# A two-layer encoder on one core: the end of a layer by token tile, a reordered first stage, two more expert weights beside the ring, attention values by pair

## What is computed

```python
h = rms_norm(x, mix_norm_g[l])
aq, ak, av, bq, bk, bv, cq, ckv, ckr, gates = split(h @ w_in[l])
x += sum_n(sigmoid(gates_n) * (branch_n(h) @ w_branch[l, n])) @ w_out[l]
x += cross_attention(rms_norm(x, cross_norm_g[l]), rms_norm(mem, mem_norm_g[l]))
x += moe(rms_norm(x, ffn_norm_g[l]))   # 32 experts, top 2 of one group of 8
```

## Time and profile before

| | us |
|---|---|
| median of three runs (lowest, highest) | 1718.87 (1715.06, 1721.05) |
| the profiled execution | 1717.54 |
| its span, first to last instruction | 1715.4 |
| TensorE busy, share of the span | 1375.3, 80% |
| VectorE, ScalarE, GpSimd busy | 531.1, 231.5, 35.0 |
| moved by DMA | 505.57 MB, 295 GB/s on average |

### The profile page before, as it was taken

The page is one execution under the profiler, slowest core; times in us unless marked ns, Lnnn a source line. Parts: engine busy times, 40 slices in busy tenths (PEclk is TensorE's granted clock), DMA queues, the critical chain, the costliest instruction groups (busy, mean ns, idle before and its releaser), DMA issues.

```text
span 1715.4 us, 18172 instructions
## 1 busy us (share of the span) xinstructions
PE 1375.3 (80%) x7588; PEld 824.1 (48%) x7588; DVE 531.1 (31%) x1042; ACT 231.5 (13%) x552; POOL 35.0 (2%) x45
## 2 busy tenths in 40 slices
PE   5999999998666556777689999999986665676665
PEld 5887688854222123232258776887542121322211
DVE  5134646435111311221121345643432211212122
ACT  2013330022000000000011144100310000000000
POOL 2000000001000000000000000000000000000000
PEclk9999999999887878798889999999998787888888
DMA  9843227445999999999995332454489999999995
GB/s 310 270 140 99 74 70 246 157 178 217 408 421 421 422 420 421 421 421 421 421 348 171 111 111 69 118 215 168 172 324 421 421 422 421 418 421 421 422 422 234
DMA packets 137925, 505.57 MB, mean 295 GB/s; under 512 B 8688, under 2 KB 80176, under 8 KB 88432
## 3 DMA queue, kind: packets, MB, share of 16 engines
q1 hardware_dynamic: 134288, 492.98, 73.8%
q0 software_dynamic: 2704, 8.22, 1.5%
q10 hardware_dynamic: 848, 3.15, 0.5%
HBM read 503.27 MB, written 1.05 MB: 294 GB/s over the span
## 4 chain that ended last, share of the span: by engine, by line
PE 55%; DMA 39%; DVE 2%; SPq 2%; issue 1%; ACT 1%; POOL 0%; DVEq 0%; ACTq 0%; POOLq 0%
DMA ring<-in_w_dram 37%; PE banks L1435 26%; PE banks L1622 6%; PE banks L1662 5%; PE banks L1441 4%; PE banks L1734 3%; SPq L487 2%; PE banks L1546 1%; PE banks L1556 1%; PE banks L1582 1%; DMA k<-in_w_xkv_dram 1%; PE banks L1542 1%; PE banks L1591 1%; PE banks L1720 1%; PE banks L1487 0%
## 5 line engine op out<-in xcount | busy, mean ns | idle before, releaser
L1622 PE MATMUL banks<-ring,v 128*32 128x512 f32 x1936 | 302.9, 771 | 188.7 <-DMA ring<-in_w_dram 180.9
L1435 PE MATMUL banks<-hT,ring 128*128 128x256 f32 (+1 forms) x1472 | 327.6, 383 | 1.9 <-ACT hT L617 1.9
L1435 PEld LDWEIGHTS banks<-hT,ring 128*128 128x128 f32 (+1 forms) x1472 | 277.5, 190 | 48.4 <-issue 5.0
L1622 PEld LDWEIGHTS banks<-ring,v 128*32 128x32 f32 x1936 | 81.8, 136 | 397.1 <-issue 393.0
L1662 PE MATMUL banks<-ring,probT 128*32 128x512 f32 x1024 | 154.5, 730 | 88.3 <-DMA ring<-in_w_dram 80.0
L1662 PEld LDWEIGHTS banks<-ring,probT 128*32 128x32 f32 x1024 | 40.8, 131 | 190.4 <-issue 179.9
L1171 DVE COPY q<-banks 128x512 f32<-128x512 f32 x16 | 11.1, 692 | 246.6 <-PE banks L1662 246.6
L1591 PE MATMUL banks<-v,h 128*128 128x128 f32 x512 | 68.5, 297 | 13.3 <-issue 11.9
L1591 PEld LDWEIGHTS banks<-v,h 128*128 128x128 f32 x512 | 65.0, 209 | 27.2 <-issue 27.2
L1167 DVE TENSOR_TENSOR prob<-banks,prob 128x512 f32<-128x512 f32 x16 | 11.1, 692 | 205.6 <-PE banks L1622 205.6
L1160 DVE TENSOR_SCALAR prob<-prob 128x512 f32<-128x512 f32 x16 | 6.8, 427 | 184.8 <-ACT prob L698 184.8
(11 more groups left out here) (261 smaller groups left out, 1282.2 us busy)
## 6 DMA issues: line engine op xcount, KB each, us to landing
ring<-in_w_dram SPq DMA_DIRECT2D x370, 1024.0 KB, 19.1
ring<-in_w_in_dram SPq DMA_DIRECT2D x52, 1024.0 KB, 11.9
ring<-in_w_branch_dram SPq DMA_DIRECT2D x8, 1024.0 KB, 5.1
ring<-in_w_out_dram SPq DMA_DIRECT2D x8, 1024.0 KB, 5.9
k<-in_w_xkv_dram POOLq DMA_DIRECT2D x4, 1024.0 KB, 17.8
ring<-in_w_branch_dram SPq DMA_DIRECT2D x8, 512.0 KB, 3.5
k<-in_w_dram SPq DMA_DIRECT2D x4, 1024.0 KB, 8.6
shared<-in_w_dram SPq DMA_DIRECT2D x4, 1024.0 KB, 6.3
```

Of the source, the lines that this page charges most:

```text
L1435: last = nc.tensor.matmul(dst, w[:, k, cols], src[:, k, :], start=k == 0, stop=k == kn - 1)
L1622: last = nc.tensor.matmul(bank[2 + m][e * CAP:(e + 1) * CAP, :], xt[:, k, e * CAP:(e + 1) * CAP], ws[e][:, r * D_EXPERT:(r + 1) * D_EXPERT ...
```

## The change

It has five parts.

1. **Layer's end.** In the last round the four products go tile by tile (tile 0 both halves, then tile 1) into four PSUM banks (`END_BANKS`), so none waits for an addition. ScalarE squares each half as it is added; 1/rms is made by the half-tile form; GpSimd multiplies `x` by the norm weight, chunk by chunk, ahead of 1/rms, and the factor is put in by ScalarE (tile 0, and the first half of tile 1) and VectorE (the second half of tile 1). The norm weight is loaded by GpSimd's queue during the first round, no longer before it.
2. **TensorE filled in the joint** between the layers: four matmuls on the identity after the products, and one after the transposes of each tile.
3. **First stage.** The identity part of the constants and both `mem` weights go first on SyncE's queue; positions, the other constants and the lambdas after three ring loads. `mem` is turned over unnormed; its norm weight is put in as a factor per partition with the copies out of PSUM, and 1/rms by a multiplication of the keys with a row (made by two more matmuls on `ones` and a diagonal) and of the values with a column. The 24 setup steps come after `hT` is copied, the values' product after the transposes of `h`. Identity matmuls stand ahead of and between the transposes of `mem`.
4. **Beside the ring** there are 9 blocks: the first two w2 blocks of the first round are added, one in `prob` and a half of `probT`, one in `gain` and `oa`. What used these tiles in that time is moved to `q1` and `v1`. SyncE's queue gets two more waits: for all products of attention, and for GpSimd's four multiplications.
5. **Values by pair.** Both query tiles of a unit are multiplied at once: 12 products of 256 columns in place of 24 of 128 in A, B and C. Odd units keep their turned probabilities in `gain`, for which reason the FFN norm weight is loaded later.

```diff
+END_BANKS = (5, 2, 0, 1)
-EXTRA = 7
+EXTRA = 9
+AHEAD = [KD + i for i in range(7)] + [2 * KD, 2 * KD + 1]
...
-        act_e, act_r, hidden = flat
+        act_e, hidden = yexp[:, 0:512], yexp[:, 512:1024]
+        extras = [[e] for e in extras]
+        extras += [[prob[:, :, :, :].rearrange("p b a n -> p (b a n)"), probT[:, 1, :, :, :].rearrange("p a b n -> p (a b n)")],
+                   [gain[:, :], oa[:, :, :].rearrange("p c n -> p (c n)")]]
+        memT = shared[:, 0:SLOT].rearrange("p (k n) -> p k n", k=KD)
...
-                  .then_inc(pos_in_s, 16)
-            sp.dma_start(con[:, :], consts[:, 0:C_STRIP]).then_inc(con_in, 16)
-            sp.dma_start(lam_all, diff_lambda.rearrange("l a d -> (l a d)").rearrange("(a n) -> a n", a=1)
-                         .broadcast_to([P, DEPTH * 4 * A_DH])).then_inc(lam_in, 16)
+            sp.dma_start(con[:, 0:C_SWAP], consts[:, 0:C_SWAP]).then_inc(id_in, 16)
+            sp.dma_start(wxk, w_xkv[0, :, 0:256].rearrange("(k p) n -> p k n", p=P)).then_inc(first_wxk_in, 16)
+            sp.dma_start(wxv, w_xkv[0, :, 256:512].rearrange("(k p) n -> p k n", p=P)).then_inc(first_wxv_in, 16)
...
+            def load_beside(l, i):
+
+                src, at = quad_source(l, 0, AHEAD[i]), 0
+                for part in extras[i]:
+                    n = part.shape[1]
+                    sp.dma_start(part.rearrange("p (k n) -> p k n", k=1), src[:, :, at:at + n]).then_inc(extra_in[i], 16)
+                    at += n
...
+                    if j == 3 and l == 0:
+                        load_tables()
                     if j == RING:
+                        sp.wait_ge(mem_made, l * 2 + 2)
                         sp.dma_start(strips, consts[:, C_STRIP:]).then_inc(strips_in, 16)
...
+                in_ring = [j for j in range(PER_QUAD) if j not in AHEAD]
+                quad_turns(0, in_ring[:RING])
...
+                load_beside(l, 3)
+                sp.wait_ge(pv_done, l * PRODUCED + PRODUCED)
+                load_beside(l, 7)
                 sp.wait_ge(projected, l * 6 + 6)
-                sp.dma_start(beside(4), quad_source(l, 0, KD + 4)).then_inc(extra_in[4], 16)
+                load_beside(l, 4)
+                sp.wait_ge(gained, l * 4 + 4)
+                load_beside(l, 8)
...
+                load_beside(l, 6)
+                quad_turns(0, in_ring[RING:])
...
+                pool.wait_ge(pv_done, l * PRODUCED + X0 // 2)
+                wait_gain_used(pool, l)
+                plain(pool)
+                load_gain(ffn_norm_g[row, :])
...
+                pool.wait_ge(slot_free, done_at(l, 0, 2 * KD + QUAD - 1))
+                plain(pool)
+                load_gain(mix_norm_g[one(following), :] if following < DEPTH else final_norm_g.rearrange("(a n) -> a n", a=1))
+                pool.wait_ge(gain_in, l * 32 + 48)
+                for c in range(4):
+                    t, half = divmod(c, 2)
+                    cols = slice(half * 512, half * 512 + 512)
+                    wait_end_added(pool, l, c)
+                    nc.gpsimd.tensor_tensor(h[:, t, cols], x[:, t, cols], gain[:, cols], ALU.mult).then_inc(end_gained, 1)
...
-                nc.scalar.activation(kx, bank[0].rearrange("p (a n) -> p a n", a=2), ACT.Copy).then_inc(kx_copied, 1)
+                    for a in range(2):
+                        last = nc.scalar.activation(memT[:, 2 * g + a, :], bank_n(g)[:, a, :], ACT.Copy,
+                                                    scale=mcol[:, 2 * g + a:2 * g + a + 1])
+                    last.then_inc(memT_act, 1)
+
+            def mem_row(l):
+
+                act.wait_ge(mem_row_made, l + 1)
+                nc.scalar.activation(mem_rstd, bank[1][:, 0:SEQ], ACT.Copy).then_inc(mem_row_copied, 1)
...
+            nc.scalar.activation(small[:, 63:64], stat[:, 8:9], ACT.Square)
             mem_squares(0)
             mem_copies(0)
-            squares(0)
-
-            act.wait_ge(setup_dve, SETUP_ANGLES)
-            nc.scalar.activation(ropes[64:96, 0, :], angles[64:96, 0, :], ACT.Sin)
-            nc.scalar.activation(ropes[64:96, 1, :], angles[64:96, 1, :], ACT.Sin)
-            nc.scalar.activation(small[:, 4:8], small[:, 0:4], ACT.Exp).then_inc(setup_act, 1)
-            mem_keys(0)
+            first_squares()
+            mem_row(0)
...
+                    if i < X0:
+                        if i == 2:
+                            wait_gain_used(act, l)
+                        if u >= 2:
+                            act.wait_ge(pv_done, l * PRODUCED + (u - 1))
+                        dst = unit_probsT(u)[:, 0:n, :, b * P:(b + 1) * P]
...
-                squares(l + 1)
+                for c in range(4):
+                    t, half = divmod(c, 2)
+                    half_squares(l, 3, t, half, hT[:, 2 * c:2 * c + 2, :].rearrange("p a n -> p (a n)"))
+                act.wait_ge(end_gained, l * 4 + 2)
+                act.wait_ge(root_step, root_done(l, 3, 0))
+                nc.scalar.activation(h[:, 0, :], h[:, 0, :], ACT.Copy, scale=rstd(0)).then_inc(normed_act, 1)
+                act.wait_ge(end_gained, l * 4 + 3)
+                act.wait_ge(root_step, root_done(l, 3, 1))
+                nc.scalar.activation(h[:, 1, 0:512], h[:, 1, 0:512], ACT.Copy, scale=rstd(1)).then_inc(normed_act, 1)
...
+                    nc.vector.tensor_scalar(mem_diag[:, t, :], ident, root[:, TT + t, 3:4], None, ALU.mult)\
+                      .then_inc(mem_diag_made, 1)
...
+                    for a in range(2):
+                        last = nc.vector.tensor_scalar(memT[:, 2 * g + a, :], bank_n(g)[:, a, :],
+                                                       mcol[:, 2 * g + a:2 * g + a + 1], None, ALU.mult)
+                    last.then_inc(memT_dve, 1)
+
+            def mem_keys(l):
+
+                dve.wait_ge(mem_row_copied, l + 1)
+                dve.wait_ge(mem_made, l * 2 + 1)
+                nc.vector.tensor_tensor(kx, bank[0].rearrange("p (a n) -> p a n", a=2),
+                                        mem_rstd.rearrange("p (a n) -> p a n", a=1).broadcast_to([P, 2, SEQ]), ALU.mult)\
+                  .then_inc(kx_copied, 1)
...
+            mem_root(0)
+            first_norm()
+            mem_keys(0)
...
-                    half, t = divmod(c, 2)
+                    t, half = divmod(c, 2) if last else (c % 2, c // 2)
                     dve.wait_ge(S["combined"], rd * 4 + (c + 1))
                     xs = x[:, t, half * 512:half * 512 + 512]
-                    nc.vector.tensor_tensor(xs, xs, bank[(5, 2)[c % 2]][:, :], ALU.add).then_inc(S["added"], 1)
...
-                nc.vector.tensor_copy(lamcur, lamt[:, row]).then_inc(layer_cols, 1)
                 copy_hT(l)
+                if l == 0:
+                    mem_values(0)
+                    set_up_tables()
...
                 for t in range(TT):
-                    dve.wait_ge(S["added"], (l + 1) * QUADS * 4 + t)
-                    norm(l + 1, (t,))
+                    half_root_start(l, 3, t)
+                    half_root(l, 3, t)
+                dve.wait_ge(end_gained, l * 4 + 4)
+                nc.vector.tensor_scalar(h[:, 1, 512:1024], h[:, 1, 512:1024], rstd(1), None, ALU.mult).then_inc(normed_dve, 1)
...
-                wait_hT(l, 0, 2)
+                    if l > 0:
+                        stay_warm(1, bank[0], C_INV)
...
+            def mem_turn(l, warm=0):
 
                 for t in range(TT):
-                    pe.wait_ge(mem_normed, l * 2 + (t + 1))
+                    if t == 1 and warm:
+                        stay_warm(warm, bank[2], C_SWAP)
...
+                features(bank[0][:, 0:SEQ], wxk, slice(0, P), memT, KD)
+                pe.wait_ge(mem_diag_made, l * TT + TT)
+                for t in range(TT):
+                    last = nc.tensor.matmul(bank[1][:, t * P:(t + 1) * P], ones, mem_diag[:, t, :], start=True, stop=True)
+                last.then_inc(mem_row_made, 1)
+                features(bank[0][:, SEQ:2 * SEQ], wxk, slice(P, 2 * P), memT, KD).then_inc(mem_made, 1)
...
+            def products(l, u):
+
+                pe.wait_ge(probsT_copied, l * NI + (2 * u + 2))
...
+                probs, dst = unit_probsT(u), bank[7][:, 0:SEQ]
+                if 2 * u < B0:
                     for c in range(TT):
-                        last = nc.tensor.matmul(dst, v0[:, c, u * P:(u + 1) * P], probT[:, i % 2, 0, c, :],
+                        last = nc.tensor.matmul(dst, v0[:, c, u * P:(u + 1) * P], probs[:, 0, c, :],
                                                 start=c == 0, stop=c == TT - 1)
                 else:
-                    v, hd = (v1, 2 * (u - 4)) if i < C0 else (v0, 2 * (u - 8)) if i < X0 else (vx, 2 * (u - 12))
+                    v, hd = (v1, 2 * (u - 4)) if 2 * u < C0 else (v0, 2 * (u - 8))
...
                     for first in range(0, QUAD, n):
-                        for e in range(first, first + n):
-                            wait(2 * KD + part * QUAD + e)
```

(34 more changed lines are left out.)

404 lines of the change are left out of this document (219 added, 185 removed).

## The result

The changed kernel takes 1698.09 us (median of four runs, 1697.21 to 1701.51), the kernel before 1719.96 (1715.06 to 1721.85): a ratio of 0.9879, 95% interval 0.9857 to 0.9901, some 21 us faster. The forecast was 1691, with a range that holds the result; 26.8 us were expected of the change. The profiled executions differ by 20.0 us in their spans (1715.4 and 1695.4), and those can be taken apart. Each stretch runs from one event to the next: start of the first projection, end of attention, SyncE's first issue in the weight stream, start of the last four products, and in layer 2 the copy of the first projection's result out of PSUM.

A forecast was written before the change was run, and what follows sets the result against it. Bound by TensorE in mixing and expert-weight DMA in the experts, with three joints where neither is busy. Terms 8.8 + 5.6 + 2.0 + 8.0 + 2.4 = 26.8 off 1717.5 gave 1691 us; range 1682 to 1702.

The forecast's parts named there:

- (a): Joint between the layers: the clock falls in spite of the fillers, 5.6 us lost, time 1697; chance 0.22.
- (b): First stage: mem's key weights still land late, at 20.3, so the stage gains 2.3 us; time 1697; chance 0.10.
- (d): Layer ends: GpSimd's multiplications are held up beside VectorE, ending 3 us behind the root; time 1697; chance 0.04.
- Weight stream, 8.8 forecast: Expert weight stream: two blocks fewer save 5.0 us a layer, less 1.2 for layer 2's norm weight; 8.8 us.
- Joint, 5.6 forecast: Joint between the layers: projections start 2.7 us earlier and the held clock saves 2.9; 5.6 us.
- a half-tile root takes 2.16: Joint: VectorE makes each half-tile 1/rms in 2.16 us, two in a row ending at 873.8 and 875.9.
- End, 2.0 forecast: End of the program: the joint's sequence without TensorE has h ready sooner; 2.0 us, bounds 1 and 2.5.
- First stage, 8.0 forecast: Start of the kernel: projections start at 30.9 against 38.89; 8.0 us, bounds 5.5 and 10.
- 14.2: First stage: time in us at which mem's key weights were taken to land, so that the keys end at about 22.
- Values by pair, 2.4 forecast: Attention: B and C units save 0.17 us each, A nothing; about 1.2 a layer, 2.4 us; bounds 0 and 5.
- (c): Weight stream: the ring runs dry or the stream starts later, by the term's 8.8 us; time 1700; chance 0.06.
- (e): Attention: pairs make TensorE wait on copies, 31 us if each of 24 pairs did; time 1724; chance 0.03.

The follow-up runs named there:

- norm weight as a row: Changed kernel with each layer end's norm weight loaded as one 4 KB row and spread by TensorE, not as a 0.5 MB copy; 1695.84 us.
- combined: Changed kernel with column loads after the first norm, mem's layer-2 column in layer 1's attention, GpSimd for tile 0 alone at layer ends; 1693.22 us, ratio 0.9851.

## Why the prediction was right or wrong

The sum was 26.8, the spans gave 20.0. That the time lies in the range says little for the mechanism: 1698 is also what rivals (a), (b) and (d) were priced at, 1697. The terms of the sum fell short by 8.6 us together, and 1.8 us came back where the sum had less or nothing (pairs, and the clock after attention); only the rows tell these apart. By its own steps:

- **Weight stream, 8.8 forecast, 6.9 measured.** "A block costs 2.49": right, or a little low (2.7). The step that failed is that the norm weights change places at no cost in layer 1 and for 1.2 in layer 2. They cost 1.9 and 2.0: the copy to 128 partitions costs 1.0 to 1.5 in layer 1 and about 1.8 in layer 2, and mem's column, which the sum didn't count at all, about 1. In layer 1 the copy takes the place of the old one of mem's norm weight, as forecast, so the column explains only about half of the 1.9; the rest stays open.
- **Joint, 5.6 forecast, 4.0 measured.** The 2.9 of the held clock came in full, and is safe only with the fillers. The schedule gave 1.1 for 2.7: "a half-tile root takes 2.16" is wrong beside GpSimd. The error was to ask only whether VectorE slows GpSimd (rival d); it is the other way, 1.6 us.
- **End, 2.0 forecast, 0.4 measured:** the same 1.6.
- **First stage, 8.0 forecast, 4.5 measured.** This is the largest miss. "14.2" for the key weights' landing was 16.5. Their wait is the rival (b), but its cause was not SyncE's poor share alone: the change sends 2048 packets of 4 bytes out 27 us earlier, past a wait that it moved. "The keys at full clock, 7.0" failed by 1.8, since the clock fell after the wait. With both mended the stage ended at 30.3 to 30.7 in three kernels, against 30.9 in the sum; h was ready at 22.3, as forecast.
- **Values by pair, 2.4 forecast, 3.3 measured.** 1.0 a unit was right. The rest is what one product fewer for each pair saves in TensorE's busy time, in A too (2.35 us a layer in all), less 0.7 of waits; where between the products it is saved was only argued.
- **Attention's end to stream**, not in the sum: 0.9 net, and it goes with the clock. Of the 28 such stretches of the fourteen executions, the clock stayed up in seven (167.2 to 167.5 us); in the others it fell between the norm and the expert products, briefly (167.5 to 167.9) or for longer (169.2 to 171.6).

Of the rivals, (c) and (e) did not come, (a) not in this execution but in three variants, (b) by 2.3 us of its 6, and (d) with its direction reversed.

## What to carry to other kernels

When a wait or load is moved in a queue, list what stood behind it and now goes earlier: here two loads of 4 KB held up the first 1 MB of weights by 1.1 us. Beside an instruction on GpSimd, price VectorE's smallest instructions that read two SBUF operands at the rest of GpSimd's one, and let the latter end first. Where TensorE waits ahead of a critical stage, fill the wait up to its end, since a gap of 2.6 to 5.2 us here cost from nothing to 2.9 us of clock behind it, from one execution to the next.

## What was not expected of the hardware

A column load of 1024 packets of 4 bytes keeps all 16 DMA engines busy while they move little (251 GB/s over 2 us with one such load; 197 over 4 us with two and gcol's smaller ones). The Trainium skill, "DMA: Bandwidth & Descriptors", Specifications, gives 512 B as the least transfer at line rate; the rows agree in that such packets fill the engines without moving bytes. A one-column instruction on VectorE took 1.30 us for 0.15 beside GpSimd. And with "norm weight as a row" a last group of products partly at 1.2 GHz, behind a wait of 2.63 us for weights, ate the 1.5 us that a shorter stream had given; in the kernel before (2.56 us) and in "combined" (2.44) the clock stayed up behind the same wait.
